# First block by halves, second steps in other banks, both gates ahead of further pieces, padding cleared by ScalarE

## Chip, core and metric

The kernel runs on one core of one Trainium2 chip. Times are microseconds of device time. The core has TensorE (PE), VectorE (DVE), ScalarE (ACT), GpSimd (POOL) and SyncE (SP), which issues most loads. A time is one execution; three were taken of the kernel before, and one more was profiled.

## The reference, cut to what matters

The input is one sequence of 256 tokens of width 1,024, float32. Two layers follow each other, then two more mixers with layer norms:

```python
def swiglu(h, w_in, w_out):
    a, b = jnp.split(h @ w_in, 2, axis=-1)
    return (jax.nn.silu(a) * b) @ w_out

h = h + 0.5 * swiglu(rmsnorm(h, ffn_norm[0, 0]), ffn_w_in[0, 0], ffn_w_out[0, 0])      # block 0
h = h + mlstm_mixer(rmsnorm(h, mix_norm[0]), ...)                                      # mlstm, mlstm_out
h = h + 0.5 * swiglu(rmsnorm(h, ffn_norm[0, 1]), ffn_w_in[0, 1], ffn_w_out[0, 1])      # block 1
kv = nsa_shared_kv(h, ...)                                                             # kv, compressed keys
h = h + 0.5 * swiglu(rmsnorm(h, ffn_norm[1, 0]), ffn_w_in[1, 0], ffn_w_out[1, 0])      # block 2
h = h + nsa_mixer(rmsnorm(h, mix_norm[1]), kv, ...)                                    # nsa, nsa_out
h = h + 0.5 * swiglu(rmsnorm(h, ffn_norm[1, 1]), ffn_w_in[1, 1], ffn_w_out[1, 1])      # block 3
# then fox and dsa, two attention mixers with layer norms
```

`ffn_w_in` of a block is 1,024 x 5,632 and `ffn_w_out` 2,816 x 1,024. The blocks are called `ffn0` to `ffn3`.

## The kernel before

**Products in parts.** Every float32 product is made from three fp32r products. An operand is split in a high part (rounded to fp32r, by ScalarE) and a low part (the rest, by VectorE); TensorE adds high x high, high x low and low x high in the same PSUM bank. For weights a *piece* is 128 x 2,048 elements (1 MB). SyncE loads it into `raw` (7 slots, which share their memory with `wlo`), ScalarE copies it to `whi` (`hi`, L1524), and VectorE makes `wlo = raw - whi` in place (`lo`, L2052). TensorE waits for `lo_done`, and the last product that reads a piece raises `used`, which frees the slot for the load seven pieces on. Both engines make pieces in a written-out order: `split_to(p)` means "all pieces below p, if not yet made". `AHEAD` is 4.

**Activations.** `turn_h` (L696) transposes a half (`w`) of a tile (`t`, 128 tokens) of the residual `h` on TensorE. ScalarE's `x_hi` (L1546, or L1549 without gains) reads it from PSUM, multiplies by the norm's gain and gives `XH`; VectorE's `x_lo` (L2092, L2099) gives `XL`. The factor of the root mean square (`rn`, by `token_root` from ScalarE's `squares`, L1538) comes in only at the gates.

**A block.** `ffn(f)` goes through 11 steps of 256 columns each of a and b. `in_half(i, t)` sums a step's 512 columns for tile t in bank 4 + t (24 products: L686, L687, L689; in the first step of block 0 L721, L722 and L728, by `first_by_piece`). ScalarE makes the sigmoid (`exps`, L1578), VectorE the gate in two operations (`silu`, L2151 and L2154), raising `gated`. `turn_g(i)` (L822) transposes the gated values into bank 6, ScalarE and VectorE make `GH` and `GL`, and `out_step(i)` multiplies them with `w_out` into banks 0 to 3 (two per tile), where the sums of all steps stay. The order on TensorE is in(0), in(1, 0), `turn_g(0)`, in(1, 1), `out_step(0)`, `turn_g(1)`, in(2) and so on. Before the sums of step i and tile t, TensorE waits for the gate of step i - 1 and tile t, because they share a bank:

```python
pe.wait_ge(gated, 2 * (n0 + i - 1) + t + 1)
```

**The start.** x's tile 0 is loaded by SyncE, tile 1, the identity and further constants by ScalarE's queue, and nine groups of parameter rows by GpSimd's. The first piece is loaded and split in two parts (`lead_in`, `lead_hi`, `lead_lo`), the second whole. ScalarE makes x tile 0 (both halves), the first piece, x tile 1, the second piece, then both tiles' squares. TensorE's L836 transposes the parameter rows between the first and the second step.

**mlstm_out.** `out_stage` multiplies tile 0, then tile 1 with four pieces of `a_w_out`, with the transposes of head outputs (`turn_heads`, L736) between them and those of `ffn1` before the last part. VectorE's `update` (L2122) adds the sums to `h`, after which `turn_h` can go.

**Block 2's side work.** Between its sums, block 2 compresses keys and values: halves `ct0` to `ct3` are transposed (L1139) and copied by ScalarE or VectorE (`shifted`, L2462 and L2463), the keys are normalised (`root("keys", 16)`, L2064 to L2074), and blocks of tokens are written to `FH` and `FL` (128 x 2,048), whose padding columns must be zero. GpSimd clears both tiles whole (L657, L659) once the transposes that used that memory are done.

## Time and profile before

| | |
|---|---|
| median of three runs | 1309.86 us (1309.32 to 1311.05) |
| profiled execution | 1311.08 us, span of its instructions 1309.3 us |
| busy share of the span | PE 97%, DVE 67%, ACT 47%, POOL 2% |
| mean granted TensorE clock | 0.992 |

The span is what the profile shows, from the first to the last instruction; the rest of the execution's time lies around it. Matmuls are pipelined and their modelled ends overlap the next start: in a running stream a product of 512 columns is 0.39 us long and the next starts 0.23 us after it.

### The profile page before, as it was taken

Reading aid. Unit: us, or ns where it says so; the run is one execution under the profiler, and the core shown is the slowest. Engines: PE = TensorE matmul, PEld = TensorE weight load, DVE = VectorE, ACT = ScalarE, POOL = GpSimd, SP = SyncE. Lnnn points to the kernel's source line nnn. Section 1 sums busy time; section 2 is a strip of 40 time slices with the busy share of each in tenths; the row PEclk is TensorE's granted clock in tenths of the full one; section 3 lists DMA queues with packets and bytes.
Section 4 is the critical chain, followed back from the end, with each engine's and each line's share of the span. In section 5 each row is a group of like instructions: output and inputs, shape, how many; then the busy total and the mean of one; then the engine's idle time right before and its main releaser. Section 6 shows DMA issues by size and latency. Waiting matters only on the chain.

```text
span 1309.3 us, 16502 instructions
## 1 busy us (share of the span) xinstructions
PE 1272.1 (97%) x6717; PEld 1079.9 (82%) x6717; DVE 875.3 (67%) x1323; ACT 613.6 (47%) x839; POOL 24.2 (2%) x37
## 2 busy tenths in 40 slices
PE   7999999999999999999999998999999999999997
PEld 5888888987888888878888886778888899988876
DVE  6655557796755557686657569856555567566896
ACT  6444436445444346444535447654444344544461
POOL 2000000100000000000000000000000000000000
PEclk9999999899999999999999989999999999999999
DMA  9655545444655555555665440065566686446401
GB/s 330 215 193 183 185 150 183 130 159 138 207 186 181 183 186 183 185 169 185 201 229 188 136 161 1 1 202 186 191 193 193 130 219 171 149 133 208 175 2 65
DMA packets 158811, 218.17 MB, mean 167 GB/s; under 512 B 8256, under 2 KB 110992, under 8 KB 158736
## 3 DMA queue, kind: packets, MB, share of 16 engines
q1 hardware_dynamic: 156880, 212.56, 51.1%
q0 software_dynamic: 1376, 3.71, 0.9%
q8 instruction: 53, 0.87, 0.3%
q10 hardware_dynamic: 480, 0.85, 0.2%
q14 instruction: 22, 0.18, 0.0%
HBM read 216.04 MB, written 1.05 MB: 166 GB/s over the span
## 4 chain that ended last, share of the span: by engine, by line
PE 81%; DVE 12%; ACT 3%; issue 2%; SPq 1%; DMA 1%; DVEq 0%
PE PS L686 23%; PE PS L687 23%; PE PS L689 23%; DVE wlo L2052 3%; PE PS L822 1%; PE PS L721 1%; PE PS L722 1%; ACT whi L1524 1%; PE PS L706 1%; PE PS L728 1%; PE PS L1015 1%; PE PS L1301 1%; SPq L591 1%; DVE arena L2648 1%; DVE XL L2092 1%
## 5 line engine op out<-in xcount | busy, mean ns | idle before, releaser
L2052 DVE TENSOR_TENSOR wlo<-raw,whi 128x2048 fp32r<-128x2048 f32 (+4 forms) x206 | 457.3, 2230 | 123.1 <-ACT whi L1524 122.3
L1524 ACT ACTIVATE whi<-raw 128x2048 fp32r<-128x2048 f32 (+4 forms) x206 | 381.4, 1863 | 63.6 <-DMA raw<-in_fox_w_in_dram 33.3
L686 PE MATMUL PS<-whi,XL 128*128 128x512 f32 (+3 forms) x992 | 384.7, 389 | 7.7 <-DVE scr L2154 2.8
L687 PE MATMUL PS<-wlo,XH 128*128 128x512 f32 (+3 forms) x992 | 378.5, 382 | 0.0
L689 PE MATMUL PS<-whi,XH 128*128 128x512 f32 (+3 forms) x992 | 263.9, 383 | 0.0
L686 PEld LDWEIGHTS PS<-whi,XL 128*128 128x128 f32 x992 | 186.4, 188 | 43.6 <-DVE scr L2154 4.0
L689 PEld LDWEIGHTS PS<-whi,XH 128*128 128x128 f32 x992 | 184.8, 189 | 35.1
L687 PEld LDWEIGHTS PS<-wlo,XH 128*128 128x128 f32 x992 | 186.6, 188 | 32.6
L1578 ACT ACTIVATE scr<-PS,rn 128x256 f32<-128x256 f32 x88 | 41.7, 474 | 225.3 <-PE PS L689 224.0
L686 PE MATMUL PS<-whi,GL 128*128 128x512 f32 x320 | 125.4, 392 | 0.0
L687 PE MATMUL PS<-wlo,GH 128*128 128x512 f32 x320 | 124.6, 389 | 0.0
L2151 DVE SCALAR_TENSOR_TENSOR scr<-PS,rn,scr 128x256 f32<-128x256 f32 x88 | 42.4, 482 | 92.8 <-ACT scr L1578 92.8
L1583 ACT ACTIVATE GH<-PS 128x512 fp32r<-128x512 f32 x40 | 23.9, 599 | 165.6 <-PE PS L822 165.6
L689 PE MATMUL PS<-whi,GH 128*128 128x512 f32 x320 | 98.7, 390 | 0.0
L686 PE MATMUL PS<-XH,wlo 128*128 128x256 f32 x320 | 83.1, 291 | 1.2 <-ACT xs L2019 1.2
L687 PE MATMUL PS<-XL,whi 128*128 128x256 f32 x320 | 81.7, 287 | 0.0
L2160 DVE TENSOR_TENSOR GL<-PS,GH 128x512 fp32r<-128x512 f32 x40 | 27.7, 692 | 77.9 <-ACT GH L1583 77.9
L689 PEld LDWEIGHTS PS<-whi,GH 128*128 128x128 f32 x320 | 60.1, 188 | 12.6
L686 PEld LDWEIGHTS PS<-whi,GL 128*128 128x128 f32 x320 | 60.1, 188 | 12.2
L687 PEld LDWEIGHTS PS<-wlo,GH 128*128 128x128 f32 x320 | 60.1, 188 | 12.1
L686 PEld LDWEIGHTS PS<-XH,wlo 128*128 128x128 f32 x320 | 62.7, 196 | 2.9 <-ACT xs L2019 2.0
L687 PEld LDWEIGHTS PS<-XL,whi 128*128 128x128 f32 x320 | 62.7, 196 | 0.1
(387 smaller groups left out, 1348.6 us busy)
## 6 DMA issues: line engine op xcount, KB each, us to landing
raw<-in_ffn_w_in_dram SPq DMA_DIRECT2D x174, 512.0 KB, 5.0
raw<-in_ffn_w_out_dram SPq DMA_DIRECT2D x88, 512.0 KB, 4.9
raw<-in_fox_w_in_dram SPq DMA_DIRECT2D x24, 512.0 KB, 7.9
raw<-in_a_w_in_dram SPq DMA_DIRECT2D x16, 512.0 KB, 4.7
raw<-in_dsa_w_in_dram SPq DMA_DIRECT2D x16, 512.0 KB, 6.1
raw<-in_kv_w_dram SPq DMA_DIRECT2D x12, 512.0 KB, 4.2
raw<-in_fox_w_in_dram SPq DMA_DIRECT2D x12, 344.0 KB, 5.1
raw<-in_a_w_out_dram SPq DMA_DIRECT2D x8, 512.0 KB, 4.8
```

Source lines behind the costliest of these rows:

```text
L591: sp.dma_start(dst[:, :, w, :], w_in[:, 4 * half:4 * half + 4, w, FC * i:FC * i + FC])\
L686: mm(o, xl, wh, start=start and i == 0, stop=False, skip_group_check=True)
L687: mm(o, xh, wl, start=False, stop=False, skip_group_check=True)
L689: last = mm(o, xh, wh, start=False, stop=stop and i == len(terms) - 1, skip_group_check=True)
L706: last = tr(PS[:, turn_bank(name, t, w), k * P:k * P + P], h[:, t, (4 * w + k) * P:(4 * w + k) * P + P], ident)
L721: mm(o, xh, wl, start=opens and i == 0 and j == 0, stop=False, skip_group_check=True)
L1524: A(whi[:, p % SLOTS, 0:n], raw[:, p % SLOTS, 0:n], ACT.Copy).then_inc(hi_done, 1)
L1578: A(ffe[:, t, :], PS[:, 4 + t, 0:FC], ACT.Sigmoid, scale=rn[:, t:t + 1]).then_inc(exp_done, 1)
L1583: A(to[:, :, :].rearrange("p k t -> p (k t)"), PS[:, 6, :], ACT.Copy).then_inc(gh_done, 1)
L2052: V.tensor_tensor(wlo[:, p % SLOTS, 0:n], raw[:, p % SLOTS, 0:n], whi[:, p % SLOTS, 0:n].bitcast(F32), ALU.subtract).then_inc(lo_done, 1)
L2151: V.scalar_tensor_tensor(out=g, in0=PS[:, 4 + t, 0:FC], scalar=rn[:, t:t + 1], in1=e, op0=ALU.mult, op1=ALU.mult).then_inc(silu_step, 1)
L2160: V.tensor_tensor(to[:, :, :], two(PS[:, 6, :]), hi_[:, :, :].bitcast(F32), ALU.subtract)\
```

## The change

- **Start.** x's tile 1 is loaded by SyncE, behind the first two of the first piece's loads; the other constants by GpSimd, behind the rows, which wait for `lead_hi` 2. The first two pieces are both loaded and split in two parts. x is made in the order tile 0 half 0, tile 1 half 0, tile 0 half 1, tile 1 half 1, between the parts of the weights (`hi_at` and `x_at` give the new counts). Tile 0's squares are made first of all. The transpose of the rows goes behind `turn_g(1)`, its copy to step 2.
- **Second steps.** In blocks 0, 1 and 3 the sums of step 1 go to banks 2 and 3 (`in_bank`), so they wait for no gate; `out_step(0)` waits for both gates of step 1 before its second tile. Step 2 in those blocks waits for the gates of step 0 only.
- **VectorE's order in a block.** In step 1 both gates come ahead of further pieces and of the side work; in step 0 the side work comes ahead of the last piece; in block 0 the piece between the two gates of step 0 goes behind them. ScalarE in block 0 makes one piece less ahead of each sigmoid of step 0.
- **mlstm_out.** ScalarE makes two pieces of `ffn1` before its x of tile 1; VectorE one before each half; one `x_lo` is put in the middle of a root.
- **Padding.** ScalarE clears the 17 padding columns of each group in `FH` and `FL` instead of GpSimd's clears of the whole tiles.

```diff
...
         landed = [sem(f"landed{r}") for r in range(SLOTS)]
-        lead_in = sem("lead_in")
+        lead_in = [sem(f"lead_in{p}") for p in range(2)]
         lead_hi = sem("lead_hi")
...
+        def hi_at(name, t, w):
+
+            if name == "ffn0":
+                return 2 * w + t + 1
+            return 4 * turns.index(name) + 2 * t + w + 1
+
         def x_at(name, t, k):
...
+            if name == "ffn0":
+                return 8 * (k // 4) + 4 * t + k % 4 + 1
             if name in whole_banks:
...
             return first_piece["ffn2"] + in_piece(2, cmp_after[kv]) + 2
+
+        def in_bank(f, i, t):
+
+            return 2 + t if i == 1 and f != 2 else 4 + t
...
                         dst = raw[:, p % SLOTS, :].rearrange("p (k w n) -> p k w n", k=4, w=2)
-                        if p == 0:
-                            for part, there in ((slice(0, 2), lead_in), (slice(2, 4), landed[0])):
+                        if p < 2:
+                            for part, there in ((slice(0, 2), lead_in[p]), (slice(2, 4), landed[p])):
                                 for w in range(2):
-                                    sp.dma_start(dst[:, part, w, :], w_in[:, part, w, 0:FC]).then_inc(there, 16)
+                                    sp.dma_start(dst[:, part, w, :], w_in[:, 4 * p + part.start:4 * p + part.stop, w, 0:FC])\
+                                        .then_inc(there, 16)
+                                if p == 0 and there is lead_in[0]:
+                                    sp.dma_start(h[:, 1, :], a["x"][0, P:T, :]).then_inc(x_in[1], 16)
                             continue
...
+            pool.wait_ge(lead_hi, 2)
             load_rows(R_MIX, 16, a["mix_norm"].rearrange("l (k p) -> (l k) p", p=P))
...
                 pool.dma_start(rowsb[R_KN:R_KN + 3, 64 * half:64 * half + 64], a["k_norm"]).then_inc(params_in, 16)
+            pool.dma_start(con[:, C_CAUS:C_ALL], a["con"][:, C_CAUS:C_ALL]).then_inc(con_in, 16)
             pool.dma_start(w2s[:, :, :, :], a["cmp_w2"].rearrange("c (k p) d -> p c k d", p=P)).then_inc(small_in, 16)
...
             pool.memset(VB[:, :, :, :], 0.0).then_inc(pads_ready, 1)
-            pool.wait_ge(side_ps, made(side_no["ct3"]))
-            pool.memset(FH[:, :, :, :].bitcast(F32), 0.0).then_inc(pads_ready, 1)
-            pool.wait_ge(side_ps, made(side_no["kt3"]))
-            pool.memset(FL[:, :, :, :].bitcast(F32), 0.0).then_inc(pads_ready, 1)
...
                 for i, (w, ks) in enumerate(banks):
-                    if los[i] == 1:
-                        pe.wait_ge(lead_lo, 1)
+                    lead = los[i] in (1, 2)
+                    if lead:
+                        pe.wait_ge(lead_lo, los[i])
                     elif los[i]:
                         pe.wait_ge(lo_done, los[i])
-                    pe.wait_ge(turned_hi, 4 * turns.index(name) + 2 * t + w + 1)
+                    pe.wait_ge(turned_hi, hi_at(name, t, w))
                     for j, (k, wh, wl) in enumerate(ks):
-                        if los[i] == 1 and j == 2:
-                            pe.wait_ge(lo_done, 1)
+                        if lead and j == 2:
+                            pe.wait_ge(lo_done, los[i])
                         xh = XH[:, k, t * P:t * P + P]
...
                             o = PS[:, 4 + t, :]
-                            first_products(o, name, t, [(half, ks)], (0 if t else p0 + half + 1,), half == 0)
+                            first_products(o, name, t, [(half, ks)], (0 if t else half + 1,), half == 0)
                             last = last_products(o, name, t, half, ks, half == 1)
...
                     p = p0 + in_piece(f, i)
-                    pe.wait_ge(gated, 2 * (n0 + i - 1) + t + 1)
+                    if i >= 2 or f == 2:
+                        pe.wait_ge(gated, 2 * (n0 + i - (2 if i == 2 and f != 2 else 1)) + t + 1)
                     for half in range(2):
...
                         wh, wl = parts(p + half, 4)
-                        last = product(PS[:, 4 + t, :],
+                        last = product(PS[:, in_bank(f, i, t), :],
                                        [(XH[:, 4 * half + k, t * P:t * P + P], XL[:, 4 * half + k, t * P:t * P + P],
...
                     last = i == NI - 1
-                    out_piece(p, 0, GHz if last else GH, GLz if last else GL, i == 0, last, then_turns[name], between)
+
+                    def second_step_read():
+                        pe.wait_ge(gated, 2 * (n0 + 1) + 2)
+
+                    out_piece(p, 0, GHz if last else GH, GLz if last else GL, i == 0, last, then_turns[name],
+                              second_step_read if i == 0 and f != 2 else between)
...
                 in_half(0, 1)
-                if f == 0:
-                    pe.wait_ge(params_in, 16 * 9)
-                    tr(PS[:, 7, 0:R_ALL], rowsb[0:R_ALL, :], con[0:R_ALL, 0:R_ALL]).then_inc(par_ps, 1)
                 in_half(1, 0)
...
                 turn_g(1)
+                if f == 0:
+                    pe.wait_ge(params_in, 16 * 9)
+                    tr(PS[:, 7, 0:R_ALL], rowsb[0:R_ALL, :], con[0:R_ALL, 0:R_ALL]).then_inc(par_ps, 1)
                 for i in range(2, NI - 1):
...
                         act.wait_ge(used, p0 + in_piece(f, i) + 2)
-                    A(ffe[:, t, :], PS[:, 4 + t, 0:FC], ACT.Sigmoid, scale=rn[:, t:t + 1]).then_inc(exp_done, 1)
+                    A(ffe[:, t, :], PS[:, in_bank(f, i, t), 0:FC], ACT.Sigmoid, scale=rn[:, t:t + 1]).then_inc(exp_done, 1)
...
                     p = p0 + in_piece(f, i)
-                    split_to(p + AHEAD + 1)
+                    split_to(p + AHEAD + (1 if f or i else 0))
                     if i == 0:
...
                         during(i, 0)
-                    split_to(p + AHEAD + 2)
+                    split_to(p + AHEAD + (2 if f or i else 1))
                     exps(1, i)
...
                         split_to(p + AHEAD + 3)
+                    else:
+                        split_to(p + AHEAD + 2)
                     g_hi(i)
...
                 .then_inc(par_in, 16)
-            act.dma_start(h[:, 1, :], a["x"][0, P:T, :]).then_inc(x_in[1], 16)
-            act.dma_start(con[:, C_CAUS:C_ALL], a["con"][:, C_CAUS:C_ALL]).then_inc(con_in, 16)
             act.wait_ge(warm_set, 1)
             A(warm[:, :], warm[:, :], ACT.Sigmoid)
+            squares("ffn0", 0)
             act.wait_ge(par_ready, 1)
-            x_hi("ffn0", 0)
-            act.wait_ge(lead_in, 32)
-            A(whi[:, 0, 0:PIECE // 2], raw[:, 0, 0:PIECE // 2], ACT.Copy).then_inc(lead_hi, 1)
-            act.wait_ge(landed[0], 32)
-            A(whi[:, 0, PIECE // 2:PIECE], raw[:, 0, PIECE // 2:PIECE], ACT.Copy).then_inc(hi_done, 1)
-            split[0] = 1
-            x_hi("ffn0", 1)
-            split_to(2)
-            for t in range(NT):
-                squares("ffn0", t)
+            x_hi("ffn0", 0, (0,))
+
+            def lead(p, part):
+
+                cols = slice(PIECE // 2 * part, PIECE // 2 * part + PIECE // 2)
+                act.wait_ge(landed[p] if part else lead_in[p], 32)
+                A(whi[:, p, cols], raw[:, p, cols], ACT.Copy).then_inc(hi_done if part else lead_hi, 1)
+
+            lead(0, 0)
+            lead(0, 1)
+            x_hi("ffn0", 1, (0,))
+            x_hi("ffn0", 0, (1,))
+            lead(1, 0)
+            x_hi("ffn0", 1, (1,))
+            lead(1, 1)
+            split[0] = 2
+            squares("ffn0", 1)
             ffn(0)
...
             x_hi("mlstm_out", 0, (1,))
+            split_to(first + 6)
             x_hi("mlstm_out", 1)
...
                 A(FH[:, :, :, 0:NCMP], v_fs, ACT.Copy).then_inc(by_act, 1)
+
+            def clear_pads(table, after):
+
+                act.wait_ge(side_ps, made(side_no[after]))
+                A(table[:, :, :, NCMP:32], zcol.unsqueeze(2).unsqueeze(3).to_broadcast([P, 16, KVH, 32 - NCMP]), ACT.Copy)\
+                    .then_inc(pads_ready, 1)
...
                     A(KTS[:, b, 0:2, :], two(o), ACT.Identity, scale=par[:, R_KN + 1 + b:R_KN + 2 + b]).then_inc(side_act, 1)
+                elif (i, t) == (2, 1):
+                    clear_pads(FH, "ct3")
                 elif (i, t) == (3, 1):
                     block_hi(0)
+                    clear_pads(FL, "kt3")
                 elif (i, t) == (5, 0):
...
-            def root(name, w, to=rr):
+            def root(name, w, to=rr, amid=None):
...
                 link(V.scalar_tensor_tensor(out=y, in0=t_, scalar=ROOT_C, in1=y, op0=ALU.add, op1=ALU.mult))
+                if amid:
+                    amid()
                 link(V.tensor_tensor(t_, y, y, ALU.mult))
...
-                dve.wait_ge(turned_hi, 4 * turns.index(name) + 2 * t + w + 1)
+                dve.wait_ge(turned_hi, hi_at(name, t, w))
                 if name in gains:
...
                         dve.wait_ge(g_turned, n0 + i)
-                    V.scalar_tensor_tensor(out=g, in0=PS[:, 4 + t, 0:FC], scalar=rn[:, t:t + 1], in1=e,
+                    V.scalar_tensor_tensor(out=g, in0=PS[:, in_bank(f, i, t), 0:FC], scalar=rn[:, t:t + 1], in1=e,
                                            op0=ALU.mult, op1=ALU.mult).then_inc(silu_step, 1)
                     dve.wait_ge(silu_step, q + 1)
-                    V.scalar_tensor_tensor(out=g, in0=PS[:, 4 + t, FC:2 * FC], scalar=rn[:, t:t + 1], in1=g,
+                    V.scalar_tensor_tensor(out=g, in0=PS[:, in_bank(f, i, t), FC:2 * FC], scalar=rn[:, t:t + 1], in1=g,
                                            op0=ALU.mult, op1=ALU.mult).then_inc(gated, 1)
...
                     silu(0, i)
-                    if during:
+                    if during and i != 1:
                         during(i, 0)
-                    split_to(p + AHEAD + 2 - late)
+                    if i != 1 and (f or i):
+                        split_to(p + AHEAD + 2 - late)
                     silu(1, i)
-                    split_to(p + AHEAD + 2)
+                    if during and i == 1:
+                        during(i, 0)
+                    if i:
+                        split_to(p + AHEAD + 2)
                     if during:
                         during(i, 1)
+                    split_to(p + AHEAD + 2)
                     if i:
                         split_to(p + AHEAD + 3)
-                    if f == 0 and i == 0:
+                    if f == 0 and i == 2:
                         dve.wait_ge(par_ps, 2)
...
             dve.wait_ge(par_ready, 1)
-            for w in range(2):
-                x_lo("ffn0", 0, w)
-            for part, there, out in ((slice(0, PIECE // 2), lead_hi, lead_lo), (slice(PIECE // 2, PIECE), hi_done, lo_done)):
-                dve.wait_ge(there, 1)
-                V.tensor_tensor(wlo[:, 0, part], raw[:, 0, part], whi[:, 0, part].bitcast(F32), ALU.subtract).then_inc(out, 1)
-            split[0] = 1
-            for w in range(2):
-                x_lo("ffn0", 1, w)
-            split_to(2)
+            x_lo("ffn0", 0, 0)
+
+            def lead(p, part):
+
+                cols = slice(PIECE // 2 * part, PIECE // 2 * part + PIECE // 2)
+                dve.wait_ge(hi_done if part else lead_hi, p + 1)
+                V.tensor_tensor(wlo[:, p, cols], raw[:, p, cols], whi[:, p, cols].bitcast(F32), ALU.subtract)\
+                    .then_inc(lo_done if part else lead_lo, 1)
+
+            lead(0, 0)
+            lead(0, 1)
+            x_lo("ffn0", 1, 0)
+            x_lo("ffn0", 0, 1)
+            lead(1, 0)
+            x_lo("ffn0", 1, 1)
+            lead(1, 1)
+            split[0] = 2
             token_root("ffn0")
...
-            def head_root(g):
+            def head_root(g, amid=None):
...
                 mean_square(8, P, EPS, ss[:, 8 * g:8 * g + 8])
-                root(f"head{g}", 8, rr[:, 8 * g:8 * g + 8])
+                root(f"head{g}", 8, rr[:, 8 * g:8 * g + 8], amid)
...
             head_sums(1)
-            head_root(1)
-            x_lo("mlstm_out", 0, 0)
+            head_root(1, lambda: x_lo("mlstm_out", 0, 0))
             heads(0, 1)
...
             heads(1, 1)
-            split_to(first + 4)
-            for w in range(2):
-                x_lo("mlstm_out", 1, w)
+            split_to(first + 5)
+            x_lo("mlstm_out", 1, 0)
+            split_to(first + 6)
+            x_lo("mlstm_out", 1, 1)
             split_to(piece_end("mlstm_out") + AHEAD - 1)
```

## Rows read from the trace of the kernel before

**Rows 1.** The page's busy times: engine, busy us, share, instructions.
```profile
PE 1272.1 (97%) x6717; PEld 1079.9 (82%) x6717; DVE 875.3 (67%) x1323; ACT 613.6 (47%) x839; POOL 24.2 (2%) x37
```

**Rows 2.** Waits of PE: who waited for whom, us, times, longest.
```profile
PE PS L686 <- DVE scr L2154: 2.8, 3, 1.1
...
PE PS L706 <- DVE h L2122: 1.6, 1, 1.6
...
PE PS L721 <- DVE wlo L2267: 1.5, 1, 1.5
PE PS L822 <- DVE scr L2154: 1.2, 1, 1.2
...
PE PS L1139 <- DVE arena L2463: 0.6, 1, 0.6
```

**Rows 3.** Timeline of the start: start, length, engine, line; idle before and releaser.
```profile
7.05 2.17 ACT L1546 ACTIVATE XH<-PS,par 128x128 fp32r<-128x128 f32 x8 [2.80 <-PE PS L706]
...
8.30 2.16 DVE L2092 SCALAR_TENSOR_TENSOR XL<-PS,par,XH 128x128 fp32r<-128x128 f32 x8 [2.18 <-ACT XH L1546]
9.06 1.11 ACT L1652 ACTIVATE whi<-raw 128x1024 fp32r<-128x1024 f32 x1
10.38 2.37 DVE L2267 TENSOR_TENSOR wlo<-raw,whi 128x1024 fp32r<-128x1024 f32 x2
10.44 1.06 ACT L1654 ACTIVATE whi<-raw 128x1024 fp32r<-128x1024 f32 x1 [0.27 <-DMA raw<-in_ffn_w_in_dram]
...
11.65 0.79 PE L721 MATMUL PS<-wlo,XH 128*128 128x512 f32 x1 [1.49 <-DVE wlo L2267]
...
15.62 1.05 ACT L1538 ACTIVATE xs<-h 128x1024 f32<-128x1024 f32 x1
```

**Rows 4.** Stretches: us, PE, PEld, DVE, ACT, POOL busy (instructions), granted clock, DMA, GB/s.
```profile
12.20:15.20 3.00, 3.00 (x8) 2.31 (x7) 2.62 (x9) 2.75 (x7) 0.00 (x0) 1.00 1.10 349
16.20:19.20 3.00, 3.00 (x15) 2.49 (x14) 2.81 (x8) 3.00 (x5) 0.00 (x0) 1.00 1.10 352
244.50:251.30 6.80, 6.80 (x33) 6.58 (x32) 6.73 (x6) 5.43 (x11) 2.57 (x2) 0.50 0.44 160
```

**Rows 5.** Timeline from the first to the second step of block 0.
```profile
20.00 4.49 DVE L2052 TENSOR_TENSOR wlo<-raw,whi 128x2048 fp32r<-128x2048 f32 x2
...
24.58 0.25 PE L836 MATMUL PS<-con,arena 101*128 101x101 f32 x1
...
25.89 0.50 PE L686 MATMUL PS<-whi,XL 128*128 128x512 f32 x1 [1.06 <-DVE scr L2154]
```

**Rows 6.** Timeline in mlstm_out, up to the first transposes of block 1.
```profile
289.13 0.47 PE L686 MATMUL PS<-whi,XL 128*128 128x512 f32 x1 [0.41 <-DVE XL L2099]
...
298.54 0.60 ACT L1549 ACTIVATE XH<-PS 128x512 fp32r<-128x512 f32 x1 [5.33 <-PE PS L736]
...
304.25 6.70 DVE L2052 TENSOR_TENSOR wlo<-raw,whi 128x2048 fp32r<-128x2048 f32 x3 [1.11 <-ACT whi L1524]
...
311.60 0.66 PE L706 MATMUL PS<-con,h 128*128 128x128 f32 x4 [1.61 <-DVE h L2122]
```

**Rows 7.** Loads issued near 327.4: KB each, us from issue to landing.
```profile
raw<-in_ffn_w_in_dram SPq DMA_DIRECT2D x2, 512.0 KB, 7.4
```

**Rows 8.** Timeline of block 2's side work.
```profile
556.68 0.63 PE L1139 MATMUL PS<-con,arena 128*128 128x128 f32 x4 [0.59 <-DVE arena L2463]
...
563.54 0.17 DVE L2064 TENSOR_SCALAR ry<-rv 128x16 uint32<-128x16 uint32 x1
563.71 1.81 POOL L657 MEMSET FH<- 128x2048 f32 x1 [244.71 <-PE PS L1139]
563.75 1.81 DVE L2065 TENSOR_SCALAR rv<-rv 128x16 f32<-128x16 f32 x1
...
570.34 0.66 PE L822 MATMUL PS<-con,scr 128*128 128x128 f32 x4 [1.22 <-DVE scr L2154]
...
600.57 1.01 ACT L1777 ACTIVATE FH<-xs 128x960 fp32r<-128x960 f32 x1
```

## Prediction

> **What bounds the kernel now.** I read the page's list of busy times first, because it says which engine has no room: TensorE's matmuls fill 97% of the span [rows 1]. So a microsecond is won only where TensorE stands still or runs slowly, and work on the others is free until TensorE waits for it. Next the waits of TensorE, longest first [rows 2]: the reader is to see that none is a queue of many equal waits; they are single stalls of 0.4 to 1.6 us at stage borders. Five groups sit at places that the diff edits: VectorE's split weights before the first product (1.5), the gates before a second step (2.8 in 3 waits: 1.06 in block 0 [rows 5], so 0.89 each in blocks 1 and 3), the residual update behind `mlstm_out` (1.6), the gates before `turn_g(1)` of block 2 (1.2), and a shifted key half (0.6). Last I read the timeline around each, to see what stands in front of the engine that is waited for.
>
> **The start, by halves.** TensorE's first product begins at 11.65, when VectorE has made the low half of the first piece's first half; ahead of that VectorE made eight low halves of x in 2.16 us, and ScalarE eight high ones [rows 3]. Four of the eight belong to x's second half, which is now made later: 4 x 2.16/8 = 1.08 us earlier. The weights allow it: they were there when ScalarE came to them at 9.06 without a wait, x's tile 1 now queues behind the first 0.5 MB of weights on SP, and 240 KB of constants leave the start. The other four of tile 0 come after tile 1's first four, in the order in which TensorE uses them. The second half of the first step needs piece 1 now in halves: by adding up VectorE's work from 10.6 (1.2 + 1.1 + 1.1 + 1.2 + 1.1 + 1.2 us, from the same rows) its last low part is there at about 17.5, where it was 18.0. The squares of tile 0 (1.05 us and the read of the sum) move into ScalarE's idle 2.80 us before 7.05, so tile 0 costs nothing. Nine row loads of GpSimd now wait for ScalarE's third lead copy, at about 13.6, and need some 5 us to issue; TensorE asks for them only after `out_step(0)`, near 40. That is 20 us of cover; without it each microsecond would be TensorE's. Their transpose (0.25 us [rows 5]) is moved, not removed.
>
> What the 1.08 us are worth depends on the pace. Eight products began in 3.0 us from 12.2 (about 0.43 us apart, the 1.2 GHz level) and fifteen from 16.2 (about 0.23 apart, 2.4 GHz); the granted clock reads 1.00 in both, so here I go by the pace [rows 4]. If the faster pace comes at the same moment as before, the time won is spent at the slow pace: 1.08/0.43 = 2.5 products, worth 2.5 x 0.227 = 0.57 us. If it comes equally soon after the first product, all 1.08 count. If it comes much sooner (the pause before the first product shrinks from 1.49 us to about 0.4), some 4 us at slow pace turn fast, 2 us more, less what piece 1 then makes TensorE wait: I cap it at 2.2. I take 1.1, bounds 0.6 and 2.2.
>
> **Second steps in banks 2 and 3.** TensorE ends the first step at about 24.6, does the row transpose, and stands 1.06 us until the first step's gate is read [rows 5]. With other banks the wait is gone: the split pieces that the second step reads are done at 24.5 [rows 5], and sooner if the start is. Gain 1.06. In blocks 1 and 3 it is (2.8 - 1.06)/2, 0.9 each [rows 2]. The wait that comes instead stands in the middle of `out_step(0)`, whose second tile writes banks 2 and 3: both gates of step 1 must be read by then. Queued behind it are the rest of that step and `turn_g(1)`. After the end of the second step's sums there is a sigmoid (0.47) and two gates (2 x 0.48) to do, 1.5 us with hand-overs, while TensorE has 12 products, 2.7 us. Before, VectorE put a 2.2 us split (4.49/2 [rows 5]) between them, which would have made this late; the diff moves both gates ahead of it. The sigmoid stands behind ScalarE's high copy of the piece seven on: in block 1 its load is issued at 327.4 and lands 7.4 us later [rows 7], 3 us before it would matter. I cost the new wait at nothing, at most 0.5 per block.
>
> **mlstm_out.** Before, ScalarE is idle 5.33 us ahead of its next high half of x, then makes three weight copies in one go; VectorE makes three low parts from 304.25 to 310.95, and only then the update that TensorE waits 1.61 us for [rows 6]. Now two of the three pieces are split in the idle time. VectorE's sum from 298.3: 2.3 (piece), 0.7 (x), 2.3, 0.7, 2.3 gives 306.6 for the update, against TensorE's arrival near 310. Gain 1.61. Its thin spot: tile 1's first x_lo now ends at 301.2, and TensorE comes at 301.5; if late, up to 0.7 is lost. The x_lo moved into the root removes a wait of 0.41 [rows 6], but TensorE next needs the piece whose low part ends at 298.3 whatever happens, so I cost that gain at 0.
>
> **Block 2.** VectorE's order of step 0 puts the shifted half ahead of a 2.2 us split, so its copies end 2.2 us earlier and the 0.59 us wait goes [rows 8]. `turn_g(1)` waits 1.22 because root arithmetic sits before the second gate, and one of its instructions on 16 columns took 1.81 us instead of 0.17, just while GpSimd cleared `FH` [rows 8]. Both causes go: the gate comes first, ScalarE clears. The 10 root steps come later, and the keys are needed at about 575: VectorE has them at 573.4. ScalarE pays two copies of 1,088 columns; the nearest row is 960 columns in 1.01 us [rows 8], so about 1.1 us each, in gaps of 3 us before the next sums. Gain 0.59 + 1.22 = 1.81, lower bound 1.2 if the keys become late.
>
> The Trainium skill's "SBUF — State Buffer", section "Who interferes with whom", says that GpSimd and a VectorE operation in a two-port mode take one shared pair of ports, and that the other fully blocks. This case's trace agrees: 1.81 against 0.17 us. By that rule ScalarE's clears block nobody; by the rows alone the sum is the same, as that stretch lies within the 1.22.
>
> **Sum:** 1.1 + 1.06 + 1.61 + 0.89 + 1.81 + 0.89 = 7.4 us. The idle times in the records leave out about 0.2 us at each restart (a product's modelled end overlaps the next start: 0.39 us long, 0.23 apart), of which I count 0.2 in all: 7.6. The profiled execution took 1311.1 us with a span of 1309.3, so it would become 1303.5; the median of the three runs is 1309.86, 1.2 lower. I predict against the median: 1302.3 us.
>
> **The rivals.**
> - The start gives nothing: with x's tile 1 in SP's queue and more, smaller loads, piece 0's second part or piece 1 lands later, and the early start ends in a wait. For it: ScalarE already waits there for a load (0.27 us [rows 3]). Against: fewer bytes are ahead. Time 1302.3 + 1.1 = 1303.4.
> - `mlstm_out` only moves its wait: x_lo of tile 1 is late twice (0.7 each) and the update late: 1303.9.
> - TensorE's clock falls or stays elsewhere. It read 0.50 for 6.8 us from 244.5 [rows 4] after idle time and small products. One such stretch more or less is worth up to half of it, 3.4 us; half that is typical: 1304.0 or 1300.6.
> - The second steps start earlier but the gates stop TensorE at `turn_g` or `out_step`: 1.06 + 2 x 0.89 + 1.22 = 4.1 us are given back: 1306.4.
> - Slower than before: the new wait in `out_step(0)`, in three blocks, behind the load of the piece seven on. It costs nothing until that load takes 3 us more than its 7.4; to end above 1312.5 it has to stall 3.4 us per block (10.2 in all), so a landing after some 13.8 us. Nothing in blocks 1 and 3 shows that.
>
> **How the numbers follow.** Forecast as summed 0.58; start lost 0.13; `mlstm_out` lost 0.10; clock stretch 0.09; gates given back 0.05; slower 0.02; the given-back gates and a lost clock stretch together, which ends within 0.2%, 0.03. The bounds of the parts give 1300.3 to 1303.9 for the forecast alone (start 0.6 to 2.2, restarts up to 0.9 in all, gates 0.5, block 2 1.2). The range that leaves out no more than 2 in 10 is 1299.8 to 1305.2. A change below 0.2% (2.6 us) can't be told from none; faster 0.95, same 0.03, slower 0.02.
>
> **What would show it.** First product at about 10.6; no idle time of TensorE before the products of any second step, save block 2's own waits; none before the transposes of `ffn1`; none above 0.2 us in the middle of `out_step(0)`; no long root instruction in block 2. Wrong would be: a first product no earlier, an idle gap before piece 1's products near 17, a new wait of `out_step(0)` on a gate, or a new half-clock stretch.

## The result, and the profile of the kernel after

The kernel after took 1299.16 us (median of four executions, 1297.56 to 1300.45) beside 1309.59 us before on the same chip: ratio 0.9923 [0.9908, 0.9939], 10.4 us faster where 7.6 were forecast. Two later sessions gave 0.9927 [0.9913, 0.9940] and 0.9918 [0.9906, 0.9931]. The profiled execution took 1297.56 us with a span of 1295.8.

The page of the kernel after, busy times, answers to [rows 1]. The span fell by 13.5 us and TensorE's busy time by 8.1 of them, though no product was taken out: what was won was only in part recorded as idle before (the rest is pace, clock and restarts, in the table below). GpSimd lost its two clears.

```profile
span 1295.8 us, 16504 instructions
PE 1264.0 (98%) x6717; PEld 1075.5 (83%) x6717; DVE 874.3 (67%) x1324; ACT 616.2 (48%) x842; POOL 21.1 (2%) x36
```

Its waits of TensorE (who for whom; us, times, longest) answer to [rows 2].

```profile
PE PS L1321 <- DVE arena L2701: 3.6, 6, 1.2
PE PS L699 <- DVE wlo L2090: 2.9, 3, 1.7
PE PS L1302 <- ACT arena L1902: 2.8, 1, 2.8
...
PE PS L735 <- DVE wlo L2314: 0.6, 1, 0.6
```

The gates (`scr`, 2.8 us in three waits and 1.2 in one) and the residual update (`h`, 1.6) are gone from the list. The first product's wait is 0.6 instead of 1.5. One entry is new, inside the second line: 0.50 us in `mlstm_out`, below.

The start of the kernel after, timeline (start, length, engine, line; in brackets the idle time before and its releaser), answers to [rows 3, 5].

```profile
8.25 1.13 DVE L2132 SCALAR_TENSOR_TENSOR XL<-PS,par,XH 128x128 fp32r<-128x128 f32 x4 [2.18 <-ACT XH L1566]
9.29 2.50 DVE L2314 TENSOR_TENSOR wlo<-raw,whi 128x1024 fp32r<-128x1024 f32 x2
9.48 1.06 ACT L1677 ACTIVATE whi<-raw 128x1024 fp32r<-128x1024 f32 x1 [0.40 <-DMA raw<-in_ffn_w_in_dram]
...
10.56 0.50 PE L735 MATMUL PS<-wlo,XH 128*128 128x512 f32 x1 [0.58 <-DVE wlo L2314]
10.89 0.40 PE L736 MATMUL PS<-whi,XH 128*128 128x512 f32 x1
...
21.98 0.39 PE L699 MATMUL PS<-whi,XL 128*128 128x512 f32 x1
```

VectorE makes four low halves where it made eight, the first product begins at 10.56 (11.65 before), and the second step begins at 21.98 with no idle time (25.89 before). That is 3.9 us, more than the first product's 1.1 and the gate's 1.06 together.

`mlstm_out` after, VectorE and TensorE, answers to [rows 6].

```profile
290.58 4.48 DVE L2090 TENSOR_TENSOR wlo<-raw,whi 128x2048 fp32r<-128x2048 f32 x2
...
292.92 0.50 PE L699 MATMUL PS<-whi,XL 128*128 128x512 f32 x1 [0.50 <-DVE wlo L2090]
...
298.85 2.29 DVE L2090 TENSOR_TENSOR wlo<-raw,whi 128x2048 fp32r<-128x2048 f32 x1 [0.39 <-ACT whi L1544]
301.06 1.28 DVE L2162 SCALAR_TENSOR_TENSOR h<-PS,h 128x512 f32<-128x512 f32 x2
...
304.43 1.03 PE L719 MATMUL PS<-con,h 128*128 128x128 f32 x8
```

The update begins at 301.06, more than 3 us ahead of TensorE, which no longer waits for it. TensorE does not wait at the thin spot that the prediction named either, but a wait of 0.50 for a low part came up at 292.92: the piece that the prediction said it would need next in any case.

Block 2 after, around the root arithmetic, answers to [rows 8].

```profile
555.26 0.48 DVE L2194 SCALAR_TENSOR_TENSOR scr<-PS,rn,scr 128x256 f32<-128x256 f32 x1
555.66 0.17 DVE L2119 TENSOR_SCALAR rv<-ss 128x16 f32<-128x16 f32 x1
...
559.63 0.60 PE L837 MATMUL PS<-con,scr 128*128 128x128 f32 x4
...
572.04 1.16 ACT L1811 ACTIVATE FH<-con 128x1088 fp32r<-128x1088 f32 x1
```

The second gate comes ahead of the root, no root instruction is long, and `turn_g(1)` does not wait. ScalarE's two clears took 1.16 us each (1.1 forecast).

**Where the time came from.** I compared both traces product by product: the start of TensorE's k-th product before minus that of the k-th after, leaving out the moved row transpose. The difference changes only at these places (the sum is 13.5, as that of the spans):

| place | trace, us | forecast, us |
|---|---|---|
| first product, 11.65 to 10.56 | 1.09 | 1.08, all in the start's term of 1.1 |
| pace of the first products | 1.51 | 0 |
| second step of block 0 | 1.31 + 0.15 | 1.06 |
| row transpose, at its new place | -0.09 | 0 |
| `x_lo` moved into the root, 289.1, given back at 298.3 | 0.65 - 0.69 | 0 |
| `mlstm_out` | 1.77 + 0.22 | 1.61 |
| block 1 | 1.05 + 0.13 | 0.89 |
| block 2 | 0.76 + 1.44 | 0.59 + 1.22 |
| block 3 | 1.05 + 0.18 | 0.89 |
| half clock: 3.4 us near 244 for 6.8, none near 760 for 3.4 | 1.46 + 1.59 | 0 |
| between 776 and 798, with half-clock stretches in both | -0.13 | 0 |

The small second figures of blocks 0, 1, 3 and `mlstm_out` are the first few products after a restart, which follow each other a little more slowly. The restart in block 1, before and then after:

```profile
328.28 0.50 PE L686 MATMUL PS<-whi,XL 128*128 128x512 f32 x1 [0.89 <-DVE scr L2154]
328.62 0.39 PE L687 MATMUL PS<-wlo,XH 128*128 128x512 f32 x1
328.85 0.40 PE L686 MATMUL PS<-whi,XL 128*128 128x512 f32 x1
```

```profile
319.83 0.39 PE L699 MATMUL PS<-whi,XL 128*128 128x512 f32 x1
320.06 0.39 PE L700 MATMUL PS<-wlo,XH 128*128 128x512 f32 x1
```

The last product of the first step starts at 327.00 before, 1.28 us ahead of 328.28; after, that distance is 0.23. So 1.05 us are won at the first product where the record has 0.89 of idle time.

### The profile page after: what moved, and what is told of

Read it like the earlier page. It is cut to its first block, busy times and chain, and to the rows that moved or that the text cites. A ratio compares the mean times of both kernels' runs of the same rounds, so it can differ in the third digit from the quotient of the medians.

```text
span 1295.8 us, 16504 instructions
## 1 busy us (share of the span) xinstructions
PE 1264.0 (98%) x6717; PEld 1075.5 (83%) x6717; DVE 874.3 (67%) x1324; ACT 616.2 (48%) x842; POOL 21.1 (2%) x36
## 3 DMA queue, kind: packets, MB, share of 16 engines
HBM read 216.04 MB, written 1.05 MB: 168 GB/s over the span
## 4 chain that ended last, share of the span: by engine, by line
PE 85%; DVE 11%; ACT 2%; issue 1%; DMA 0%; SPq 0%; DVEq 0%
PE PS L699 24%; PE PS L700 24%; PE PS L702 24%; DVE wlo L2090 2%; PE PS L735 2%; PE PS L736 2%; PE PS L742 2%; PE PS L837 1%; PE PS L719 1%; PE PS L1321 1%; PE PS L1035 1%; ACT whi L1544 1%; DVE arena L2701 1%; DMA raw<-in_ffn_w_in_dram 0%; PE PS L1336 0%
## 5 line engine op out<-in xcount | busy, mean ns | idle before, releaser
L699 PEld LDWEIGHTS PS<-whi,GL 128*128 128x128 f32 x320 | 60.1, 188 | 12.2
```

Source lines behind the costliest of these rows:

```text
L699: mm(o, xl, wh, start=start and i == 0, stop=False, skip_group_check=True)
```

## The experiments

Theories at this point. **A:** the start's extra comes from TensorE's pace: whatever puts it at full pace before the first product would give 1.4 to 2 us. **B:** the extra comes with the early second step, once start and banks act together. **C:** each restart removed is worth more than the idle time in the records.

**The kernel before once more.** 

> The kernel before, unchanged, for a second profile. Theory A (the pace at the start is set by how long TensorE paused before its first product): it starts again at the slow pace, products about 0.43 us apart for some 4 us, and the second step of block 0 starts at 25.9. Rival B (it is chance which pace the start gets): the products may as well start 0.23 us apart, and the second step then starts near 24.4.

It took 1308.8 us. The first product stood at 11.63, nine products followed at the slow pace and the full pace came at 15.6, as in [rows 4]. The half-clock stretches had moved: 6.8 us from 756.3 and 3.4 from 776.8, none near 244. So where these stretches lie is a matter of the single execution, and the 3.0 us of the table's line on them are not the change's.

**The kernel after once more.** 

> The changed kernel, unchanged, against the kernel before. Theory A: its products start 0.23 us apart again from the first one at 10.6, the second step of block 0 starts at 22.0, and the time is 10 us below the kernel before. Rival B: a start at the slow pace is as likely; then the second step starts at 23.4 or later. The half-clock stretches of the middle (244, 760 us) differ from execution to execution in both theories.

It took 1299.27 us (1297.79 to 1299.53), ratio 0.9927 [0.9913, 0.9940]. This time six products were slow; the second step began at 22.62.

**Products on zeros ahead of the start**, in the kernel before and in the kernel after:

```diff
+            pe.wait_ge(warm_set, 2)
+            for _ in range(8):
+                mm(PS[:, 3, :], XL[:, 2, 0:P], XL[:, 0:2, :].rearrange("p k t -> p (k t)"), start=True, stop=True,
+                   skip_group_check=True)
...
+            V.memset(XL[:, 0:4, :].bitcast(F32), 0.0).then_inc(warm_set, 1)
```

> The kernel before, with one memset and eight products of zeros added ahead of the first transpose (their results are not used). Theory A: TensorE is busy before its transposes, so its full pace is there at the first product: 4 us at slow pace turn fast, 1.4 to 2 us less than the kernel before, 1307.5 to 1308.2. Rival B: the pace is chance or hangs on something else: no difference, or 0.5 us slower if the eight products delay the transposes.

> The changed kernel with the same eight products of zeros ahead. Theory A, if the changed kernel starts at full pace anyway: no difference to it (1299). Rival B, if its start is fast only by chance: 0.5 to 1.5 us less than the changed kernel in the median, and a narrower spread.

Neither did anything: 0.9999 [0.9990, 1.0008] for the first, and 0.9931 [0.9918, 0.9943] for the second, against 0.9927 of its neighbour without them. Stretches of the kernel before with zero products (us, busy PE, PEld, DVE, ACT and POOL with instructions, granted clock, DMA share, GB/s):

```profile
5.70:8.70 3.00, 2.08 (x17) 1.73 (x17) 0.93 (x4) 1.99 (x8) 2.13 (x4) 1.00 1.06 376
8.70:11.20 2.50, 0.35 (x4) 0.12 (x2) 2.50 (x7) 2.18 (x4) 0.00 (x0) 1.00 1.12 347
11.30:12.50 1.20, 1.19 (x4) 0.67 (x4) 1.20 (x2) 1.20 (x6) 0.00 (x0) 1.00 1.05 276
12.50:15.90 3.40, 3.39 (x8) 2.71 (x9) 2.52 (x9) 3.20 (x5) 0.00 (x0) 0.50 1.10 349
16.20:19.20 3.00, 3.00 (x14) 2.44 (x14) 2.76 (x10) 3.00 (x5) 0.00 (x0) 1.00 1.10 353
```

The full pace was there for the transposes (eight in 1.09 us, where the kernel before takes 1.97) and for the first four products. After TensorE's 2.5 nearly empty microseconds the clock fell to 0.50 at 12.5, with the products running, and came back at 15.9, when it had come before. In the kernel after, the half clock lay from 8.9 to 12.3 and four products were slow. Theory A, in the form "warm it and it stays", is refuted.

Nor do the zero products explain the pattern. Four profiles from below have the old start and no zero products (new banks, ScalarE's clears, block 2's order and `mlstm_out`'s part, each alone), and in all four the first two to five products follow at full pace and the clock then reads 0.50, from 12.2 to 13.2 on until 15.7 to 16.7. The one with the new banks:

```profile
9.30:12.60 3.30, 1.47 (x7) 0.80 (x6) 3.30 (x7) 3.23 (x9) 0.00 (x0) 1.00 1.10 323
12.70:16.00 3.30, 3.30 (x8) 2.62 (x9) 2.42 (x9) 2.91 (x4) 0.00 (x0) 0.50 1.10 348
```

**Parts alone.** The start (smaller loads and splits, by halves, row loads behind them):

```diff
+            x_lo("ffn0", 0, 0)
+            lead(0, 0)
+            lead(0, 1)
+            x_lo("ffn0", 1, 0)
...
-            for w in range(2):
-                x_lo("ffn0", 0, w)
...
+            pool.wait_ge(lead_hi, 2)
```

> The kernel before with the start's part alone. Theory: the first product comes 1.1 us earlier, and the slow pace ends about 2.5 us after it instead of 4.1 us or more, so the gate wait before the second step of block 0 begins 1.1 to 2.5 us earlier. Because the sigmoid of step 0 still comes before the gate, and the piece between the gates of step 0 is now behind them, the gain holds to the second step: 1.1 to 3.0 us in all. Rival, that the gate chain (root, piece, gate) and not the products set the second step's start: below 0.6 us.

Ratio 1.0002 [0.9991, 1.0012]: nothing that shows, in an interval from 1.2 us faster to 1.6 slower. TensorE in its trace:

```profile
10.51 0.79 PE L735 MATMUL PS<-wlo,XH 128*128 128x512 f32 x1 [0.40 <-DVE wlo L2292]
...
24.78 0.50 PE L699 MATMUL PS<-whi,XL 128*128 128x512 f32 x1 [1.56 <-DVE scr L2176]
```

The first product is 1.14 us earlier, as the change makes it, and fewer products were slow (seven); but the second step begins only 1.11 us earlier, because its wait for the first step's gate grew from 1.06 to 1.56. The gate took 0.50 of what the pace gave.

The second steps' banks, once with both gates ahead of the further piece and once with VectorE's old order:

```diff
-                        last = product(PS[:, 4 + t, :],
+                        last = product(PS[:, in_bank(f, i, t), :],
...
-                    split_to(p + AHEAD + 2 - late)
+                    if i != 1 or f == 2:
+                        split_to(p + AHEAD + 2 - late)
```

(the last three lines are left out in the second one)

> The kernel before with banks 2 and 3 for second steps and both gates ahead of the piece, nothing else. Theory (a stop costs its recorded idle time and about 0.2 us of restart, and the wait in the middle of out_step(0) costs nothing): the second steps of blocks 0, 1 and 3 start 1.3, 1.1 and 1.1 us earlier, 3.5 us in all. Rival (idle time alone counts): 2.8 us. Rival (the new wait stops TensorE): an idle time before the seventh product pair of out_step(0), and less than 2.5 us.

> The same banks, but VectorE keeps the piece between the two gates of step 1. Theory: the second gate ends about 2.2 us later, some 3.5 us after the sums of step 1, and TensorE asks for it 2.7 us after them: 0.7 to 1.0 us of idle time in the middle of out_step(0) of blocks 1 and 3 and up to that in block 0, so 2 to 3 us of the gain go and 0.5 to 1.5 us are left. Rival: the gates are in time either way, and the time is that of the kernel with both gates first.

With the new order 1305.4 us, ratio 0.9975 [0.9966, 0.9984]; its trace gains 1.4, 1.2 and 1.2 us at the three second steps and TensorE does not stop in `out_step(0)`. With the old order 1309.28 us, 1.0003 [0.9992, 1.0013], and this in the timeline, VectorE first, then TensorE:

```profile
36.35 2.28 DVE L2062 TENSOR_TENSOR wlo<-raw,whi 128x2048 fp32r<-128x2048 f32 x1
38.55 0.48 DVE L2161 SCALAR_TENSOR_TENSOR scr<-PS,rn,scr 128x256 f32<-128x256 f32 x1
39.06 0.48 DVE L2164 SCALAR_TENSOR_TENSOR scr<-PS,rn,scr 128x256 f32<-128x256 f32 x1
```

```profile
39.60 0.50 PE L690 MATMUL PS<-whi,GL 128*128 128x512 f32 x1 [0.64 <-DVE scr L2164]
```

A 2.28 us split stands ahead of the gate. TensorE stands idle for 0.64 to 0.66 us in each of the three blocks, and 0.94 to 0.98 us of each block's 1.2 to 1.4 are given back. The wait that the prediction costed at nothing in the new order is real in the old one; the order of the gates is what hides it.

Padding cleared by ScalarE, alone, and block 2's order of gates, alone:

```diff
-            pool.memset(FH[:, :, :, :].bitcast(F32), 0.0).then_inc(pads_ready, 1)
...
+                A(table[:, :, :, NCMP:32], zcol.unsqueeze(2).unsqueeze(3).to_broadcast([P, 16, KVH, 32 - NCMP]), ACT.Copy)\
+                    .then_inc(pads_ready, 1)
```

```diff
+                    if f == 2 and i < 2:
...
+                        silu(1, i)
+                        if i == 1:
+                            during(1, 0)
```

> The kernel before with the padding cleared by ScalarE, nothing else. Theory (the root's long instruction, 1.81 us beside GpSimd's clear, is what makes the second gate of block 2 late): no root instruction above 0.3 us, the second gate 1.6 us earlier, the idle 1.22 us before turn_g(1) gone or below 0.2; 1.2 to 1.4 us in all. Rival (the order of VectorE alone makes it late): the idle time stays above 1 us.

> The kernel before with VectorE's new order in block 2 alone; GpSimd still clears. Theory (either edit is enough for turn_g(1), as the gate then stands ahead of the root): the idle 1.22 us is gone and the 0.59 us before ct2's transposes too, 1.8 to 2.2 us in all, while the long root instruction stays at 1.8 us and costs nothing. Rival: the root, 1.6 us longer than without the clear, now makes the keys late and TensorE waits before kt0 near 574.

The first gave 0.9991 [0.9982, 0.9999] (1.1 us), the second 0.9979 [0.9970, 0.9988] (2.4 us). Both remove the wait of `turn_g(1)`, and either trace gains 1.45 us there; the order gains 0.79 more at the shifted key half. So one of the two edits is enough for `turn_g(1)`: beside the new order, no run shows a gain of ScalarE's clears. VectorE's root arithmetic in the kernel before (once more), with ScalarE's clears, and with GpSimd's clear but the new order:

```profile
560.83 1.84 DVE L2065 TENSOR_SCALAR rv<-rv 128x16 f32<-128x16 f32 x1
560.91 1.77 DVE L2067 TENSOR_SCALAR ry<-ry 128x16 int32<-128x16 int32 x1
```

```profile
563.73 0.17 DVE L2070 TENSOR_SCALAR rv<-rv 128x16 f32<-128x16 f32 x1
563.82 0.17 DVE L2072 TENSOR_SCALAR ry<-ry 128x16 int32<-128x16 int32 x1
```

```profile
561.53 1.83 POOL L657 MEMSET FH<- 128x2048 f32 x1 [243.96 <-PE PS L1139]
```

```profile
561.90 0.48 DVE L2151 SCALAR_TENSOR_TENSOR scr<-PS,rn,scr 128x256 f32<-128x256 f32 x1 [0.68 <-ACT scr L1578]
562.42 0.48 DVE L2154 SCALAR_TENSOR_TENSOR scr<-PS,rn,scr 128x256 f32<-128x256 f32 x1
562.82 0.56 DVE L2079 TENSOR_SCALAR rv<-ss 128x16 f32<-128x16 f32 x1
```

The long instruction is gone when GpSimd doesn't clear. In the third case the two gates run inside GpSimd's 1.83 us at their usual 0.48, and only the TENSOR_SCALAR behind them waits, until the clear ends at 563.36. The Trainium skill's "SBUF — State Buffer", section "Who interferes with whom", names `tensor_scalar` among the operations that can enter a two-port mode and then contend with GpSimd for a shared pair of ports. The traces agree: 1.84, 1.77 and 0.56 us beside the clear, 0.17 without it.

The part in `mlstm_out` (pieces in the idle time, and the `x_lo` moved into the root, which is left out below), alone:

```diff
+            split_to(first + 6)
             x_hi("mlstm_out", 1)
...
-            split_to(first + 4)
-            for w in range(2):
-                x_lo("mlstm_out", 1, w)
+            split_to(first + 5)
+            x_lo("mlstm_out", 1, 0)
+            split_to(first + 6)
+            x_lo("mlstm_out", 1, 1)
```

> The kernel before with the part in mlstm_out alone. Theory: 1.9 us (1.61 idle, the rest restart); the wait of 0.41 before tile 0's products goes and comes back 9 us later, ahead of the fourth piece's products, as in the changed kernel. Rival (that wait is won only together with other parts): more or less than 1.6 to 2.1.

Ratio 0.9981 [0.9972, 0.9991]. The trace gains 1.98 at the transposes of `ffn1`; the moved `x_lo` gains 0.66, and 0.66 is lost at a new wait of 0.49 for a low part, as in the kernel after.

**The loads of x's tile 1 and the constants put back on ScalarE's queue**, in the kernel after (GpSimd's row loads wait for nothing there):

```diff
-                                if p == 0 and there is lead_in[0]:
-                                    sp.dma_start(h[:, 1, :], a["x"][0, P:T, :]).then_inc(x_in[1], 16)
...
+            act.dma_start(h[:, 1, :], a["x"][0, P:T, :]).then_inc(x_in[1], 16)
```

> The changed kernel, but x's tile 1 and the constants are loaded by ScalarE's queue at the start again and GpSimd's rows wait for nothing. Theory (the new load order matters little, since ScalarE came late to the weights): the first product at 10.6 as in the changed kernel, the second piece's parts land about 1 us later, and the time is within 0.5 us of the changed kernel. Rival (the load order is what makes the start possible): the first product or the second piece's products wait for a load, 1 us or more lost.

ScalarE in its trace, for the first piece's two parts:

```profile
8.90 1.06 ACT L1675 ACTIVATE whi<-raw 128x1024 fp32r<-128x1024 f32 x1 [0.42 <-DMA raw<-in_ffn_w_in_dram]
10.77 1.06 ACT L1675 ACTIVATE whi<-raw 128x1024 fp32r<-128x1024 f32 x1 [0.82 <-DMA raw<-in_ffn_w_in_dram]
```

The first product fell back to 11.27: without the new order of loads 0.7 of the start's 1.1 us would not be there. Ten products were slow, and the second step began at 24.50, as late as without the new start (below). The time, 1299.72 us (0.9927 [0.9915, 0.9939]), can't be told from the kernel after.

**The new wait in `mlstm_out` taken out**, in the kernel after, by making the piece's low part ahead of the second heads:

```diff
+            split_to(first + 4)
```

> The changed kernel, with VectorE's fourth piece of mlstm_out ahead of the last four head products instead of behind. Theory (the 0.50 us idle in mlstm_out is this piece's low part, ended 1.1 us late): the idle time goes, 0.5 to 0.6 us less than the changed kernel, seen in the trace more surely than in the time. Rival: the head products come late for the last transposes and TensorE waits there instead, no gain.

> The changed kernel with the fourth piece ahead of the last head products, again beside the changed kernel: idle time in mlstm_out gone, 0.6 to 0.75 us less in the trace, 0 to 1.5 us less in the time.

The wait is gone in both traces. The first of them gains 0.74 us there against the kernel after and loses 0.32 again at the next half; in both, about 0.4 us are kept. The times, 1298.07 us (0.9921 [0.9909, 0.9933]) and 1297.65 us (0.9914 [0.9901, 0.9928]), are not separated from the kernel after, 0.9918 in the second one's session.

**The change without its start, beside the whole change a third time.** The edit takes back the hunks of the start alone:

```diff
-            x_lo("ffn0", 0, 0)
...
+            for w in range(2):
+                x_lo("ffn0", 0, w)
```

> The changed kernel without the part at the start (loads, order of x, pieces in halves, place of the row transpose as before). Theory (the start is worth little alone, where the gate of step 0 holds the second step back, and more where that gate is off the path): the second step of block 0 starts at 24.5 instead of 22.0 to 22.6, and the time is 1.5 to 2.5 us above the changed kernel, near 7.7 us below the kernel before. Rival (the start is worth nothing in the time, as its lone run showed): the same time as the changed kernel.

> The changed kernel again, on the same chip as the two beside it: 9 to 10.5 us below the kernel before, the first products at either pace.

Without the start 1300.24 us (1299.9 to 1300.6), 0.9933 [0.9920, 0.9947]; with it 1297.54 us (1297.36 to 1299.94), 0.9918 [0.9906, 0.9931]. The intervals overlap. The single executions fall in two groups: three of 1297.4 and 1297.5 us stand 2.0 to 2.6 below the two of 1299.5 and 1299.9. That the groups are the two paces of the start is not shown, since only the execution of 1299.51 was profiled and half-clock stretches move the time by as much. Its pace, stretches as in [rows 4], and below it that of the first profile of the same kernel (1297.56 us):

```profile
12.20:15.20 3.00, 3.00 (x8) 2.34 (x7) 3.00 (x9) 3.00 (x9) 1.22 (x3) 1.00 1.10 349
16.20:19.20 3.00, 3.00 (x14) 2.45 (x14) 2.69 (x12) 2.89 (x4) 3.00 (x7) 1.00 1.09 367
```

```profile
12.20:15.20 3.00, 3.00 (x15) 2.47 (x14) 3.00 (x10) 3.00 (x8) 1.36 (x3) 1.00 1.10 348
16.20:19.20 3.00, 3.00 (x15) 2.47 (x14) 2.65 (x13) 2.88 (x4) 3.00 (x7) 1.00 1.09 363
```

One and the same program ran 8 products in three microseconds in one execution and 15 in another. Slow products (about 0.43 us apart), and start of the second step, over all profiles with banks 2 and 3:

| kernel | slow products | second step at |
|---|---|---|
| after, three profiles | 0, 6, 12 | 21.98, 22.62, 24.22 |
| after with the wait in `mlstm_out` out, two | 0, 0 | 21.96, 21.79 |
| after with zero products | 4 | 22.46 |
| after with the old loads | 10 | 24.50 |
| after without the start | 9 | 24.55 |
| before with the new banks; with VectorE's old order too | 8, 10 | 24.37, 24.59 |

The three with none have one longer distance early on, 0.49, 0.42 and 0.32 us, at full pace before and behind it. Between the first and the third profile of the kernel after lie 2.24 us: the first product is 0.22 later, and the pace makes 2.0. So the start is worth 0.3 us in the one case and 2.6 in the other.

## Why the prediction was right in its places and too small in its sum

**Right:** the first product (1.08 forecast, 1.09 found), each of the five stalls removed, no idle time ahead of a second step nor in `out_step(0)`, the `x_lo` in the root that gives nothing, the clears on ScalarE (1.1 forecast, 1.16 found), GpSimd's late row loads (TensorE did not wait for them). None of the rivals with a loss came: no load was late enough, no gate stopped TensorE at `turn_g`.

**First failed step: "about 0.2 us at each restart ..., of which I count 0.2 in all".** The recorded idle times of the stalls sum to 1.06 + 1.61 + 0.89 + 1.81 + 0.89 = 6.26 us; the traces gained 1.46 + 1.99 + 1.18 + 2.20 + 1.23 - 0.09 = 7.97 at those places. That is 1.71 more over six restarts, 0.29 each. The rows have most of it: a product's modelled end lies 0.39 after its start, while the next would have started 0.23 after it, so 0.16 us of standing still are drawn as busy; and the second product after a restart starts 0.33 us after the first instead of 0.23 (328.28 to 328.62 above), 0.10 more. I had named the first and had both in the rows, and counted them once instead of six times. With 6 x 0.29 the sum is 9.1, the forecast 1300.7.

The other kernels bear it out. The one with the new banks alone gained 1.4, 1.2 and 1.2 us in the trace where idle times of 1.06, 0.89 and 0.89 went, and the one with `mlstm_out`'s part alone 1.98 where 1.61 went. The kernel without the start has all six restarts, and its time is 6.9 to 10.5 us below the kernel before: if the half-clock stretches even out over the executions, the idle times' 6.26 lie outside that, the traces' 7.97 inside. Theory C stands. The bound "restarts up to 0.9 in all" was too low for the same reason; besides, the stated bounds of the parts add up to 1300.5 at the low end and not to 1300.3.

**Second failed step: the start's term, 1.1, capped at 2.2.** The cases that I wrote (the pace comes at the same moment: 0.57; much sooner: up to 2.2) were the right ones, but I took them for three possible answers of the kernel, and they are different executions of one program. The third profile is the first case (full pace at 15.9, 0.3 us won), the first profile is the last (full pace from the first product, 2.6 us, above the cap of 2.2). The low end of 1299.8 was built with both bounds too tight.

**What the start needs.** Alone it showed nothing in the time. Inside the change the medians of one session differ by 2.7 us (1300.24 beside 1297.54); by the three ratios of the kernel after against 0.9933 it is 0.8 to 2.0 us, with intervals that overlap. The alone-kernel's trace shows one reason: the wait for the first step's gate, which the banks take out of the way, grew from 1.06 to 1.56 us. That supports theory B for 0.5 us; the rest of the difference lies within the spread of the times and is not shown. The prediction added its parts as independent; here two of them were not.

**Sum against time.** First product and restarts (1.09 + 7.97), without any pace or clock, give 9.1 us; with the faster pace 10.6. The three measurements say 10.4, 9.6 and 11.2. That the first of them, 10.4, comes near the sum with the faster pace agrees with its profiled execution, but in which case its other executions ran is not recorded, nor where their half-clock stretches lay.

**Open:** what decides the pace at the start. Within the new start the idle time before the first product doesn't: 0.58, 0.92 and 0.99 us went with no slow product, 0.67 with twelve, 0.2 with six. But over all profiles there is a difference between the starts. In the nine with 1.49 to 2.25 us of idle time ahead of the first product, all with the old start, the full pace that lasted came at 15.6 to 16.7 and never sooner; in the eight with 0.02 to 1.14 us, all with the new one (once with the old loads), it came anywhere from 9.2 to 16.0. So an early full pace appeared only with the new start. Whether the shorter idle time is the cause, or something else in the start, no run separates. Zero products ahead of the start did not settle it either.

## What to carry to other kernels

Price a stall of TensorE by the start-to-start distance of its products, not by the idle time in the records: here each restart cost 0.29 us more, 1.7 us over six. An earlier start is worth what the next gate lets through, so try it together with whatever holds the second step. When a bank is freed by using another, look for the wait that the new sharing makes, and put what it waits for ahead of long work on its engine (2.28 us of splitting cost 0.94 to 0.98 per block).

## What the runs showed of the hardware

- The same program starts at either pace: 0, 6 or 12 of its first products were 0.43 us apart, and the rest 0.23. The granted clock in the records reads 1.00 over both, so the pace has to be read from the distances.
- Full pace ahead of a nearly empty stretch of 2.5 us did not last: the clock went to 0.50 at 12.5, 1.2 us after the products had begun again. Four kernels without the zero products did the same at 12.2 to 13.2.
- Stretches of 3.4 and 6.8 us at clock 0.50 in mid-kernel (from 241 to 251 and from 750 to 787) move from execution to execution of the same kernel. Each 3.4 us cost 1.5 us near 244 and 1.6 near 760.
- A GpSimd memset of 1.8 us holds a VectorE TENSOR_SCALAR of 0.17 us for its whole length, and two SCALAR_TENSOR_TENSORs that read PSUM took their usual 0.48 us beside such a memset.
